# Thirty-two more pairs of SwiGLU tiles by seven block products, with their token sums in the chunk ahead

## The reference

```python
mod = (silu(c) @ ada_w[i] + ada_b[i])          # 6 x 1024 numbers a layer, for sample and prompt
h = modulate(rms_norm(x, norm1_w[i]), mod[0], mod[1]); x = x + mod[2] * mixer(h)
h = modulate(rms_norm(x, norm2_w[i]), mod[3], mod[4])
g, u = jnp.split(h @ ffn_in_w[i], 2, axis=-1)   # 1024 -> 2 x 2816
x = x + mod[5] * ((silu(g) * u) @ ffn_out_w[i]) # 2816 -> 1024
```

## Time and profile before

| | |
|---|---|
| time, median of 3 runs | 2639.33 us (2639.11 to 2639.50) |
| profiled execution | 2641.69 us, its span 2639.70 us |
| TensorE | busy 2622.5 us, 17,398 matmuls, full clock |
| VectorE | busy 1814.8 us, 69% |
| ScalarE | busy 886.7 us, 34% |
| POOL | busy 213.4 us, 8% |
| DMA | 321.41 MB, mean 122 GB/s |

### The profile page before, as it was taken

The page is one execution under the profiler, slowest core; times in us unless marked ns, Lnnn a source line. Parts: engine busy times, 40 slices in busy tenths (PEclk is TensorE's granted clock), DMA queues, the critical chain, the costliest instruction groups (busy, mean ns, idle before and its releaser), DMA issues.

```text
span 2639.7 us, 44971 instructions
## 1 busy us (share of the span) xinstructions
PE 2622.5 (99%) x17398; PEld 2551.5 (97%) x17398; DVE 1814.8 (69%) x3097; ACT 886.7 (34%) x1330; POOL 213.4 (8%) x297
## 2 busy tenths in 40 slices
PE   9999999999999999999999999999999999999998
PEld 5999999999999999999967999999999999999998
DVE  5888778676586776846676668768465557748475
ACT  4223331222342222124675432221242234425253
POOL 0000000000000000000000000000000015113020
PEclk9999999999999999999999999999999999999999
DMA  8444445444224454422101245444222224547362
GB/s 308 146 143 138 133 128 176 128 158 143 77 77 128 150 161 124 155 72 74 57 13 73 80 128 160 151 127 152 70 82 72 72 76 112 164 125 187 110 166 76
DMA packets 100025, 321.41 MB, mean 122 GB/s; under 512 B 11712, under 2 KB 14912, under 8 KB 99648
## 3 DMA queue, kind: packets, MB, share of 16 engines
q1 hardware_dynamic: 65776, 211.23, 24.6%
q0 software_dynamic: 34128, 108.54, 14.7%
HBM read 301.12 MB, written 2.88 MB: 115 GB/s over the span
## 4 chain that ended last, share of the span: by engine, by line
PE 94%; DVE 3%; DMA 1%; ACT 1%; issue 1%; DVEq 0%; POOL 0%; SPq 0%; ACTq 0%; POOLq 0%
PE ps L720 40%; PE ps L719 40%; PE ps L772 7%; PE ps_x L1018 1%; PE ps_sum L772 1%; PE ps L994 1%; PE ps L1150 1%; PE ps_sum L1005 1%; DMA mix<-in_ada_head 1%; DVE w_lo L1717 1%; PE ps L1101 0%; PE ps L875 0%; ACT w_hi L1218 0%; PE ps_sum L980 0%; DMA rope<-raw 0%
## 5 line engine op out<-in xcount | busy, mean ns | idle before, releaser
L1717 DVE TENSOR_TENSOR w_lo<-raw,w_hi 128x1024 fp32r<-128x1024 f32 (+2 forms) x319 | 383.1, 1201 | 464.3 <-ACT w_hi L1218 463.1
L1218 ACT ACTIVATE w_hi<-raw 128x1024 fp32r<-128x1024 f32 (+2 forms) x319 | 329.3, 1032 | 917.8 <-PE ps L720 902.8
L719 PE MATMUL ps<-h_hi,w_hi 128*128 128x320 f32 x1568 | 490.6, 313 | 1.3 <-DVE h_lo L2035 0.7
L720 PE MATMUL ps<-h_lo,w_hi 128*128 128x322 f32 x1568 | 489.1, 312 | 0.0
L720 PE MATMUL ps<-h_hi,w_lo 128*128 128x322 f32 x1568 | 488.0, 311 | 0.0
L719 PE MATMUL ps<-h_lo,w_hi 128*128 128x320 f32 x1568 | 487.8, 311 | 0.0
L719 PE MATMUL ps<-h_hi,w_lo 128*128 128x320 f32 x1568 | 487.5, 311 | 0.0
L720 PE MATMUL ps<-h_hi,w_hi 128*128 128x322 f32 x1568 | 486.5, 310 | 0.0
L1745 DVE CUSTOM_DVE_ANT_0 ps_x<-ada_w,cond 128x1024 f32<-128x1024 f32 x354 | 436.0, 1232 | 33.5 <-DVE tmp L1793 13.0
L720 PEld LDWEIGHTS ps<-h_hi,w_hi 128*128 128x128 f32 x1568 | 297.8, 190 | 0.6
L719 PEld LDWEIGHTS ps<-h_hi,w_hi 128*128 128x128 f32 x1568 | 296.0, 189 | 2.4 <-DVE h_lo L2035 0.8
(11 more groups left out here) (239 smaller groups left out, 4014.6 us busy)
## 6 DMA issues: line engine op xcount, KB each, us to landing
raw<-in_weights SPq DMA_DIRECT2D x323, 512.0 KB, 3.6
ada_w<-in_ada_w POOLq DMA_DIRECT2D x177, 512.0 KB, 3.8
raw<-in_weights SPq DMA_DIRECT2D x32, 384.0 KB, 3.0
rope<-in_weights SPq DMA_DIRECT2D x40, 256.0 KB, 3.2
rope<-raw POOLq DMA_DIRECT2D x40, 256.0 KB, 4.1
mix<-in_ada_head SPq DMA_DIRECT2D x16, 512.0 KB, 10.5
raw<-raw POOLq DMA_DIRECT2D x20, 256.0 KB, 3.3
x<-in_x SPq DMA_DIRECT2D x8, 320.0 KB, 10.2
```

Of the source, the lines that this page charges most:

```text
L719: pe.matmul(ps[:, 2 * slot, 0:TA], w[:, slot, ws], a(k)[:, 0:TA], start=begin, stop=end)
L720: mm = pe.matmul(ps[:, 2 * slot + 1, 0:width - TA], w[:, slot, ws], a(k)[:, TA:width], start=begin, stop=end)
L1218: act.activation(w_hi[:, j % 2, 0:tiles * P], raw[:, j, 0:tiles * P] if src is None else src, ACT.Copy).then_inc(w_hi_ready, 1)
L1717: dve.tensor_tensor(w_lo[:, j % 2, 0:tiles * P], raw[:, j, 0:tiles * P] if src is None else src, w_hi[:, j % 2, 0:tiles * P].bitcast(F32), ...
```

## The change

Engines other than TensorE have their order by hand, so turning chunks into seven products touches all of them:
- `FIRST_SEVEN` becomes [2, 2, 0, 0]: layers 0 and 1 do their third chunk by seven products, layer 2 all chunks (its first two pairs stay plain). That is 32 pairs more: 6, 6, 20.
- In layers 0 and 1 the token sums are computed in chunk 1: T1 is split in its quads' third, T2 in the first out-projection quad behind it, T3 and T4 at the start of chunk 2. POOL computes T1 between the loads of the first two triples of that chunk, and T2 to T4 behind its fourth. Layer 2 does as layer 3.
- The modulation sums are dealt out anew (`IN_ADA`, `OUT_ADA`): none within a seven-product chunk; layer 2's first plain quad keeps one triple, its out-projections two a quad (the last one); 10 triples go to layer 3's conv and its out-projection (`ADA_CONV`), one to layer 3's first plain quad. `conv` of layer 3 is now written out like layer 0's. `out_quad` may wait for single gate tiles (`kept`), and gains are made when their own tiles are there.
- POOL issues the first pair's sums of a chunk behind the third triple of the out-projection ahead.
- The rope table is loaded in front of the attention, since the pairs of layers 0 and 1 use its place.

The diff, cut to its core:

```diff
-FIRST_SEVEN = [3, 3, 3, 0]
+FIRST_SEVEN = [2, 2, 0, 0]
+IN_ADA = [[1, 1, 0], [1, 1, 0], [0, 0, 0], [0, 0, 0]]
+OUT_ADA = [[(2, 2), (1, 1)], [(2, 2), (2, 2)], [(2, 2), (2, 1)], [(0, 0), (0, 0)]]
+ADA_CONV = {0: ADA_HEAD, 3: -(-(3 * ADA_T + 2 * KD - ADA_PE) // ADA_N)}
+CONV_TRIPLES = Q_ZU + 2 * Q_B + Q_OUT
+
+
+def _in_triples(layer, c):
+    share = IN_ADA[layer][c]
+    if FIRST_SEVEN[layer] == 0 and c == 0:
+        return 1
+    return sum(share) // (2 * ADA_N) if isinstance(share, list) else share * Q_IN
+
+
+def _ada_at(layer, c, out=0):
+
+    if layer == 3:
+        return ADA_CONV[3] + CONV_TRIPLES
+    before = sum(_in_triples(n, i) + sum(OUT_ADA[n][i]) for n in range(layer + 1) for i in range(2) if n < layer or i < c)
+    return ADA_HEAD + CONV_TRIPLES + before + (_in_triples(layer, c) + sum(OUT_ADA[layer][c][:out - 1]) if out else 0)
...
+                        if LAYER_S[layer]:
+                            sp.wait_ge(block_lo_ready, SEVEN * LAYER_S[layer])
+                            sp.wait_ge(s4_made, LAYER_S[layer])
+                        load_consts(((rope, "rope", late_in),))
+                        sp.wait_ge(ada_step, 2 * ADA_N * _ada_at(layer, 0))
...
+            def sums_of_chunk(layer, c, q, n):
+                share = IN_ADA[layer][c] if isinstance(IN_ADA[layer][c], list) else []
+                def load_for(p):
+                    at, end = sum(share[:p]), sum(share[:p + 1])
+                    for tile in range(-(-at // 2), -(-end // 2)):
+                        load_ada(_ada_at(layer, c) + tile // ADA_N, tile % ADA_N)
+                load_for(0)
                 for p in range(n):
+                    if p or c == 0:
+                        sums_of_pair(layer, c, p, q)
+                    load_for(p + 1)
+            def outs_and_first_pair(layer, c, q):
+                outs = OUT_ADA[layer][c]
+                for i in range(sum(outs)):
+                    if i == outs[0] + 1:
+                        sums_of_pair(layer, c + 1, 0, q)
+                    ada_triple(_ada_at(layer, c, 1) + i)
+                if sum(outs) <= outs[0] + 1:
+                    sums_of_pair(layer, c + 1, 0, q)
+            with pool.Fori(ADA_CONV[0], ADA_CONV[0] + CONV_TRIPLES) as i:
...
+                q, kind, n = LAYER_Q[layer] + Q_MIX[KIND[layer]], KIND[layer], 2 * layer + 1
+                first = FIRST_SEVEN[layer]
+                if layer == 3:
+                    with pool.Fori(ADA_CONV[3], ADA_CONV[3] + CONV_TRIPLES) as i:
+                        for j in range(ADA_N):
+                            load_ada(i, j)
                 if kind == "attn":
                     pool.wait_ge(mixed_done, HEADS)
+                loose = 2 if first == 3 else max(first - 1, 0)
+                if loose:
+                    with pool.Fori(_ada_at(layer, 0), _ada_at(layer, loose)) as i:
+                        for j in range(ADA_N):
+                            load_ada(i, j)
+                if first == 3:
                     continue
+                if first:
+                    t = _ada_at(layer, first - 1)
                     if kind == "pool":
                         pool.wait_ge(spread_done, KD)
                     pool.wait_ge(shift_ready, n + 1)
+                    for half in range(2):
+                        ada_triple(t + half)
+                        t1_of(layer, 2 * half)
+                        t1_of(layer, 2 * half + 1)
+                    ada_triple(t + 2)
+                    ada_triple(t + 3)
                     for k in range(HALF):
                         t234_of(layer, k)
+                    outs_and_first_pair(layer, first - 1, q + first * (Q_IN + Q_OUT))
                 else:
                     if kind == "attn":
+                        ada_triple(_ada_at(layer, 0))
                     pool.wait_ge(shift_ready, n + 1)
+                    for k in range(HALF):
+                        t1_of(layer, k)
                     for k in range(HALF):
                         t234_of(layer, k)
+                        if layer == 3 and k < ADA_N:
+                            load_ada(_ada_at(layer, 0), k)
+                for c in range(first, 3):
                     qc = q + c * (Q_IN + Q_OUT) + (PLAIN_PAIRS // 2 if c == 0 else 0)
+                    sums_of_chunk(layer, c, qc, SEVENS[c])
+                    if c < 2:
+                        outs_and_first_pair(layer, c, q + (c + 1) * (Q_IN + Q_OUT))
...
+                    turning = c + 1 == FIRST_SEVEN[layer] and not edge
+                    with act.Fori(1 if late else 0, count - (1 if edge else 2 if turning else 0)) as i:
                         ffn_in_quad(i + q, i, 2 * i + r)
+                    if turning:
+                        ffn_in_quad(q + 2, 2, r + 4, turns=(layer, 1))
+                        ffn_in_quad(q + 3, 3, r + 6)
...
-                    dve.wait_ge(ada_kept, ADA_HEAD + Q_ZU + 2 * Q_B if layer == 0 else ada_before(layer, GATE2))
+                    dve.wait_ge(ada_kept, ada_before(layer, (GATE1, GATE2)[which]))
...
+                    if kept:
+                        dve.wait_ge(ada_kept, -(-(ADA_T * layer + KD * GATE2 + m + 1 - ADA_PE) // ADA_N))
...
-                        if ada:
-                            at = sum(ADA_ZU[:4 * i + j])
-                            ada_share(ADA_HEAD, at, at + ADA_ZU[4 * i + j])
+                        at = sum(ADA_ZU[:4 * i + j])
+                        ada_share(ada, at, at + ADA_ZU[4 * i + j])
...
+                for i in range(Q_ZU):
+                    zu_quad(i)
...
+                gain_of(layer, 1)
...
+                             ada=ada + Q_ZU + 2 * Q_B + half, turns=(layer, 1) if half and seven else None)
...
+                def plain_chunk(c):
+                    at = _ada_at(layer, c) if IN_ADA[layer][c] else None
+                    def ffn_in(i, norm=None, turns=None):
+                        ffn_in_quad(i + q, i, 2 * i + g, 2 * i + pr, 2 * i + r, ada=None if at is None else i + at, norm=norm, turns=turns)
+                    late, turning = c == 0 and kind == "pool", c + 1 == FIRST_SEVEN[layer] < 3
                     if late:
                         ffn_in(0, norm=2 * layer + 1)
                     elif c == 0:
                         inverse_rms(2 * layer + 1)
+                    with dve.Fori(1 if late else 0, Q_IN - 2 if turning else Q_IN) as i:
                         ffn_in(i)
+                    if turning:
+                        ffn_in(2, turns=(layer, 1))
+                        ffn_in(3)
                 for c in range(2):
                     if c < FIRST_SEVEN[layer]:
+                        plain_chunk(c)
                     elif c:
+                        seven_chunk(layer, c, q, CHUNK, pr, g, CHUNK)
                     else:
                         inverse_rms(2 * layer + 1)
+                        ffn_in_quad(q, 0, g, pr, r, tiles=(KD, KD, 0, 0), first=(layer, 0, q + 1), turns=(layer, 2),
+                                    ada=_ada_at(layer, 0))
+                        seven_chunk(layer, 0, q + 1, CHUNK - PLAIN_PAIRS, pr + PLAIN_PAIRS, g + PLAIN_PAIRS, CHUNK)
                     q += Q_IN
+                    for half, triples in enumerate(OUT_ADA[layer][c]):
+                        ahead = half and c + 1 >= FIRST_SEVEN[layer] and FIRST_SEVEN[layer] < 3
+                        out_quad(q + half, 4 * half, 0, gate_of(GATE2), (KD, KD, 0, 0) if ahead else (KD,) * 4, False,
+                                 ada=_ada_at(layer, c, half + 1) if triples else None, triples=triples,
+                                 first=(layer, c + 1, q + Q_OUT) if ahead else None,
+                                 turns=(layer, 2) if half == 0 and c + 1 == FIRST_SEVEN[layer] < 3 else None,
+                                 kept=c == 0 and FIRST_SEVEN[layer] == 0)
```

141 lines of the change are left out of this document (35 added, 106 removed).

## The result

| | before | after |
|---|---|---|
| median (runs) | 2639.41 us (4; 2639.11 to 2642.30) | 2621.73 us (4; 2618.95 to 2624.18) |
| profiled execution, its span | 2641.69, 2639.70 | 2618.95, 2617.2 |

The ratio is 0.9931 [0.9915, 0.9947]: 17.7 us faster by the medians, 22.7 by the two profiled executions. Forecast were 33.4 us, 2605.9 us, with a range of 2592 to 2619; the sign was right, the size was not, and the median lies outside the range.

A forecast was written before the change was run, and what follows sets the result against it. TensorE, busy 99% of the span, was taken as the bound, so fewer matmul columns save time. Gains of 52.6 us less costs of 19.2 gave 33.4 net, from 2639.33 to a median of 2605.9 us; 8-in-10 range 2592 to 2619.

The forecast's parts named there:

- The gains: Layers 0 to 2: 32 pairs go from 96 to 84 matmuls, 12.50 us a pair; 52.6 us saved with the out-projections.
- I count nothing: Chunk ahead and its out-projection: 32 POOL token-sum operations, 36 us, and eight turned rows per engine were to cost nothing.
- The cover that it named: Each unit leaves VectorE the 7.1 us of the next before TensorE needs the bank, so late rows seldom stall TensorE.
- a stall in the second chunk of layers 0 and 1: Listed among the signs that would show the forecast wrong; no size given.
- the second rival: POOL and VectorE in turns: layer 3's twelve sums at 2.2 us, 3 us in layers 0 and 1; 2616 to 2625, chance 0.14.
- The turn of layer 3: Modulation sums moved into layer 3's out-projection and first plain quad delay TensorE by 9.1 us, bounds 2 and 16.
- The walk: Layer 3's out-projection timeline with sums added: row 7's fold 5.9 us of stall, first evacuation 6.8 us late.
- The starts of the chunks: TensorE waits for VectorE: 3.6 us in layer 1's last chunk, 1.1 layer 0's, 1.8 layer 2's first quad, 0.6 its second chunk.
- The pair sums: DMA sums landing late: one of 20 layer 3 pairs stood 1.90 us; 32 more at that rate cost 3.0, bounds 0 and 8.
- The change acted: Answers the rival that the change doesn't act, a lookup leaving chunks plain: 2639 us, chance 0.02.
- the slower case: Pair sums by DMA become the bound, each of 32 pairs standing 1.9 us, 61 us lost: 2664 us, chance 0.05.

The follow-up runs named there:

- the filled version: Changed kernel plus useless TensorE products at its stalls in layers 1, 2 and 3, places set right in a second try; one execution, 2615.2 us.
- the versions with moved triples: Changed kernel with layer 3's last three modulation triples moved to its first chunk and the projection behind (2606.2 us), or also fourth-quad triples of layers 0 to 2 (2604.90).

## Why the prediction was wrong, point by point

Gains in us, forecast and by the stretches of the two profiled executions; the idle times of the late pairs (five after, one before) are taken out of their stretches.

| step | forecast | measured |
|---|---|---|
| last chunk of layer 0 | 9.3 | 9.1 |
| last chunk of layer 1 | 6.8 | 5.9 |
| layer 2: first, second, last chunk, projections | 5.0, 13.3, 10.4, 0.6 | 3.8, 12.7, 10.3, 0.6 |
| layer 3: turn and first chunk | -9.1 | -12.5 |
| token sums in the chunk ahead | 0 | -3.3 |
| pair sums by DMA | -3.0 | -4.4 |
| sum | 33.4 | 22.4 (with 0.3 in layer 1's mixer) |

- **The gains were right.** A pair by seven products takes 12.50 us where nothing is late; layer 3's conv took its sums at no cost (171.92 us before and after; TensorE idle at no point in the 164.9 us shown above, VectorE busy 149.4). The pairs removed 384 matmuls. The part of the sum with the gains, 52.6 us, is met to a few tenths where no stall stands.
- **"I count nothing" for the token sums** is the step that failed in kind. The prediction put no price on what POOL's additions do to VectorE's other operations in layers 0 and 1. The cover that it named, 7.1 us of a unit, hides a late row, but what was late was not a row: with POOL adding, VectorE's sums, weight split and scaling ahead of the split of the last gated tile run long, and unit 1 of the projection needs that tile. It is 1.7 us a layer in this profile, 3.0 in others. POOL's twenty additions, reckoned at 23 us, ran 29 us (531.7 to 560.7), since they are drawn out too. The prediction's own list of wrong signs, "a stall in the second chunk of layers 0 and 1", came near (the stall stands in the projection behind it), and so did the second rival at 3 us; the sum didn't. Zeros instead of sums take it to nothing.
- **The turn of layer 3** had the right mechanism and too small a term: 12.5 us instead of 9.1, within its bounds of 2 to 16. The price of a modulation sum was not at fault. 1.6 us was taken with its read-out; the twelve sums there took 1.65 on average, from 1.35 to 2.07, since POOL's operations waited for some of them and some ran when POOL was done. The walk was good as far as row 7: its fold ended 6.6 us later than before, counted from the start of the mixer's out-projection, forecast 5.9. Between it and the first evacuation the one sum was counted at 0.9, but a sum of 1.90, an addition of 0.66 and a split of 2.45 (1.89 before) stand there: 8.8 us late, forecast 6.8. The plain quad and the first blocks added 3.7 instead of 2.3. Of that the lower clock may be 1.3 us, by the filled version's one execution; the sum had no term for it.
- **The starts of the chunks** were close: the fifth block of layer 1 came 9.6 us behind the unit (forecast 9.8). They cost 4.6, 1.4, 3.0 and 1.2 us, in the order layer 1, layer 0, layer 2's first, layer 2's second, for 3.6, 1.1, 1.8 and 0.6. Each is a little more than forecast, 3.1 us in all.
- **The pair sums** were reckoned by "1 of 20 pairs". The rate was drawn from the wrong population: the late one was the fourth of a chunk of six, and the change makes such chunks out of four more stretches. It was 4.4 us in the profile. One wait aimed at it gave 9.6 us by the medians in the changed kernel, but 2.6 and 3.3 in the versions with moved triples, and what the slower executions lost to it no trace shows. That the sum of a pair and the load of the next meet was in the trace before, in SyncE's queue; the prediction doesn't use it. The port rule says nothing of this; the Trainium skill has a sentence that does ("DMA: Bandwidth & Descriptors", "SWDGE vs HWDGE vs iDMA"): queues of POOL and of SyncE feed the same engines, which take turns between them. The trace agrees in direction: here a 256 KB sum went from 3.3 us to 4.4 to 7.2.
- The profiled pair shows 11 us less than forecast. The other 5 of the 15.8 between 2605.9 and 2621.7 stand between profile and median, by the luck of which execution was profiled: the profiled execution of the kernel after was the fastest of its four, that of before 2.3 over its median. Which pairs were late in the slower ones no trace shows.
- **The rivals.** "POOL and VectorE in turns" (0.14; 2616 to 2625) named the step that failed, and its range holds the median. But its total is met by luck: it had 11 us more in layer 3, from sums of 2.2 us, where 3.4 more were measured and the sums took 1.65; its 3 us for layers 0 and 1 were right (3.3). The rest of the miss are the chunks' starts, the late pairs and the 5 us between profile and median, which it doesn't speak of. The change acted; the slower case was far.

## What to carry to other kernels

When work is moved to a second engine, price all of the first engine's operations beside it, not only those that are moved, and hold the sum against the idle time that is left: here modulation sums and token sums cost 12 us together, and each alone next to nothing. When a rate is taken from a trace, ask which instance was late and what it met there. A load and a sum that collide are better parted by one wait at the place where they meet than by a wait everywhere; what the wait gives depends on the rest of the schedule (9.6, 3.3 and 2.6 us in three versions), since the meeting can move to the next pair.

## What the runs showed of the hardware

- An accumulating DMA of 256 KB within SBUF took 3.3 to 4.7 us (median 3.4, 83 cases) with no unit load issued near it, and 4.4 to 7.2 us (median 5.4, 21 cases) where 512 KB loads went out from 1.9 us ahead of it to 0.7 us behind, in the two profiles of the changed kernel. In other versions the first kind reached 5.5 us and the second 8.1.
- VectorE's sum of 1024 columns takes 1.22 to 1.24 us alone. Beside POOL's additions it took 1.22 to 1.98 us, median 1.73 (59 cases in the same two profiles), a split of 1024 columns up to 2.94, and POOL's addition of 322 columns 0.87 to 1.97. Beside POOL's writes of zeros the sum took 1.23 (5 cases). The reciprocal, with one operand, stayed at 4.14.
- Behind idle times of TensorE of 1.8 to 4.4 us the granted clock often stood at 0.50 for 3.4 or 6.8 us, but not each time: behind the same idle time of 3.0 us once it fell and once it didn't, and behind 2.64 us it stayed up in the kernel with moved triples and in the one with zeros. It cost 1.5 us in a projection bound by TensorE, and where VectorE set the pace from nothing measurable to 1.3.
